# Two transformer blocks on one core: the adaLN weight tiles join the weight stream, the attention pipeline gets one unit deeper, and transposed probabilities alternate between two PSUM banks

## The reference, cut to what matters

```
for i in range(DEPTH):                                   # 2 layers
    m_lat = (jax.nn.silu(c) @ ada_w[i] + ada_b[i])[:, None, :]
    m_ctx = jax.nn.silu(c_ctx) @ ada_w[i] + ada_b[i]
    sh1, sc1, g1, sh2, sc2, g2 = jnp.split(m_lat, 6, axis=-1)
    h = _rms(x, norm1_g[i]) * (1.0 + sc1) + sh1          # the same for ctx
    # layer 0: Fourier mix and window attention (8 heads); layer 1: neighbourhood attention (16 heads)
    x = x + g1 * o
    h = _rms(x, norm2_g[i]) * (1.0 + sc2) + sh2
    x = x + g2 * _swiglu(h, ffn_w_gate[i], ffn_w_up[i], ffn_w_down[i])
```

## Time and profile before

| | us |
|---|---|
| three runs | 3373.81, 3312.71, 3373.85 (median 3373.81) |
| the profiled execution | 3314.83 |
| its span, first to last instruction | 3312.9 |
| PE busy | 3073.7 (93%) |
| DVE, ACT busy | 1651.8 (50%), 1531.3 (46%) |
| mean granted clock | 0.911 |

### The profile page before, as it was taken

One profiled execution on the slowest core, in us unless ns is written; L12 is line 12 of the kernel. 1 busy time (PEld: TensorE's weight loads), 2 busy tenths in 40 slices (PEclk: granted clock), 3 DMA queues, 4 the chain that ended last, 5 costly groups with the idle time before them and its releaser, 6 DMA issues.

```text
span 3312.9 us, 56503 instructions
## 1 busy us (share of the span) xinstructions
PE 3073.7 (93%) x22864; PEld 2946.2 (89%) x22864; DVE 1651.8 (50%) x2222; ACT 1531.3 (46%) x1890; POOL 332.9 (10%) x416
## 2 busy tenths in 40 slices
PE   6889998999999999999899978999999899999998
PEld 5777997799998789998899967999999899998998
DVE  5754445354454344474444685445444444644543
ACT  5754544355454245344354455534444454343552
POOL 0000210011002101021211000100000011204020
PEclk9986998599997579999999898998999899899899
DMA  8941543035446225543445312553323155334352
GB/s 313 334 155 52 177 178 127 1 139 180 157 147 126 15 82 185 181 163 114 153 152 178 139 53 89 181 184 131 115 99 131 52 175 180 140 128 143 137 188 104
DMA packets 65327, 470.07 MB, mean 142 GB/s; under 512 B 7584, under 2 KB 7584, under 8 KB 8736
## 3 DMA queue, kind: packets, MB, share of 16 engines
q1 hardware_dynamic: 63648, 464.85, 39.0%
q0 software_dynamic: 1536, 3.15, 1.6%
HBM read 466.92 MB, written 1.05 MB: 141 GB/s over the span
## 4 chain that ended last, share of the span: by engine, by line
PE 89%; DVE 6%; ACT 2%; DMA 1%; issue 1%; POOL 0%; SPq 0%; POOLq 0%; DVEq 0%; ACTq 0%
PE ps L487 18%; PE ps L488 18%; PE ps L489 18%; PE ps L667 5%; PE ps L515 5%; PE ps L517 4%; PE ps L516 4%; PE ps L696 4%; PE ps L553 3%; PE ps L678 3%; PE ps L530 2%; DVE cv L1468 2%; PE ps L557 1%; PE ps L807 1%; PE ps L536 1%
## 5 line engine op out<-in xcount | busy, mean ns | idle before, releaser
L1146 DVE TENSOR_TENSOR w_lo<-w_raw,w_hi 128x2048 fp32r<-128x2048 f32 x435 | 1001.7, 2303 | 879.4 <-ACT w_hi L871 878.6
L871 ACT ACTIVATE w_hi<-w_raw 128x2048 fp32r<-128x2048 f32 x437 | 835.6, 1913 | 490.7 <-PE ps L489 454.9
L487 PE MATMUL ps<-H_hi,w_hi 128*128 128x256 f32 x3424 | 985.7, 288 | 44.1 <-DVE H_lo L1220 13.5
L488 PE MATMUL ps<-H_lo,w_hi 128*128 128x256 f32 x3424 | 982.4, 287 | 0.0
L489 PE MATMUL ps<-H_hi,w_lo 128*128 128x256 f32 x3424 | 981.7, 287 | 0.0
L487 PEld LDWEIGHTS ps<-H_hi,w_hi 128*128 128x128 f32 x3424 | 671.6, 196 | 54.8 <-issue 34.2
L488 PEld LDWEIGHTS ps<-H_lo,w_hi 128*128 128x128 f32 x3424 | 671.5, 196 | 0.0
L489 PEld LDWEIGHTS ps<-H_hi,w_lo 128*128 128x128 f32 x3424 | 670.7, 196 | 0.0
L487 PE MATMUL ps<-A_hi,w_hi 128*128 (+1 forms) x1488 | 416.4, 280 | 27.2 <-POOL A_lo L1533 15.4
L488 PE MATMUL ps<-A_lo,w_hi 128*128 (+1 forms) x1488 | 415.0, 279 | 0.0
L489 PE MATMUL ps<-A_hi,w_lo 128*128 (+1 forms) x1488 | 414.7, 279 | 0.0
(11 more groups left out here) (196 smaller groups left out, 3437.5 us busy)
## 6 DMA issues: line engine op xcount, KB each, us to landing
w_raw<-weights_dram SPq DMA_DIRECT2D x437, 1024.0 KB, 4.8
bias_raw<-rel_bias_dram POOLq DMA_DIRECT2D x32, 96.0 KB, 5.9
consts<-consts_in_dram SPq DMA_DIRECT2D x1, 3010.0 KB, 10.0
Y<-ctx_in_dram SPq DMA_DIRECT2D x1, 1024.0 KB, 12.0
X<-x_in_dram SPq DMA_DIRECT2D x1, 1024.0 KB, 14.1
out_dram<-X SPq DMA_DIRECT2D x1, 1024.0 KB, 3.8
params<-params_in_dram SPq DMA_DIRECT2D x1, 361.0 KB, 3.2
```

The source lines that it names most:

```text
L487: mm(out, whi[:, cols], hi, start=first, stop=False, skip_group_check=True)
L488: mm(out, whi[:, cols], lo, start=False, stop=False, skip_group_check=True)
L871: return nc.scalar.activation(*a, **k)
L1146: V.tensor_tensor(w_lo[:, slot, :], w_raw[:, slot, :], whole(w_hi)[:, slot, :], ALU.subtract).then_inc(lo_done, 1)
```

## The change

Three edits, and one that goes with them.

1. The 48 ada tiles are no longer a phase of their own. Eight stand at the start (`ada`, `count=8`), enough for the first two sections of layer 0. The other 40 are put between other tiles of the stream: 8 in the context `qkv`, 8 in the context `attend`, 11 in the context `ffn_a`, 5 in the latent `qkv`, 8 in the latent `attend`. `ada_end` adds the bias for the sections that are complete, in three places.
2. An ada tile is no longer split. PE multiplies `w_raw` itself in float32, 8 products of 256 columns with 32 stationary columns, four of them into four separate groups of 32 PSUM partitions (`ada_rows_of`), and the two products that turn the rows now have 128 rows (`ada_cols_of`). The slot of `w_raw` is free when these products end. ACT's copy (`ada_row_of`) has 128 partitions instead of 4.
3. `attend` gets one unit deeper: scores(i), turn_p(i-2), weigh(i-3), with three buffers of `prob`, eight of `small`, ACT's copy ahead of its exponential, and `probT` of the dilated attention in `Y`. In the context, window and neighbourhood attention `turn_p(u)` writes bank 4 + u % 2 and waits for the copy of unit u-2 instead of u-1.
4. The loops of `in_loop` and `gemm_b` and `ffn_a` on PE are written out.

The core of the diff:

```diff
-        add("ada", l=l)
-        at["t"] += 24
-        at["ada"] += 1
+    add("ada", count=8)
+    stream(*[("ada", 0)] * 8)
+    add("ada_end", l=0, sections=(0, 1), which=0)
     for who in ("ctx", "lat"):
+        ctx = who == "ctx"
         norm(who, "ada", l=0, which=0)
-        qkv([("f", 0), ("f", 1), ("q", 0), ("q", 1), ("k", 0)], which="ev", who=who)
+        qkv([("f", 0), ("f", 1), ("q", 0), ("q", 1), ("k", 0)], lambda o: ("ev_in", o),
+            (1, 2, 1, 2, 2) if ctx else (1, 1, 1, 1, 1), which="ev", who=who)
         add("fourier")
         at["fo"] += 4
-        attend("ev", 16, who=who, banks=2)
-        gemm_b("H", 8, "gate", who=who, l=0, g=2)
+        attend("ev", 16, with_ada=8, who=who, banks=2)
+        if ctx:
+            add("ada_end", l=0, sections=(2, 3, 4, 5), which=1)
+        gemm_b("H", 8, "gate", ("ev_out", 0), who=who, l=0, g=2)
         norm(who, "ada", l=0, which=1)
-        ffn()
-        gemm_b("A", FC, "gate", who=who, l=0, g=5)
+        ffn("ffn0", 11 if ctx else 0)
+        gemm_b("A", FC, "gate", ("ffn0", FC), who=who, l=0, g=5)
+    add("ada_end", l=1, sections=range(6), which=None)
     norm("ctx", "ada", l=1, which=0)
...
-        c_wide = over("c_wide", 0, [P, C, P], F32R)
-        ada_rows = over("ada_rows", 8, [4, RING, 256])
+        c_wide = over("c_wide", 58, [P, C, 32])
+        ada_rows = over("ada_rows", 56, [P, 2, 256])
...
-        prob_a = over("prob", 48, [P, 2, 3 * T])
+        prob_a = over("prob", 48, [P, 3, 2 * T])
...
+        prob_d = over("prob_d", 56, [P, 3, 3 * T])
+        probT_d = Y[:, 0:6, :].rearrange("p (u c) t -> p u (c t)", u=2)
...
         def in_loop(eng, n, step):
 
-            full = n // RING if n >= 2 * RING else 0
-            if full:
-                with eng.Fori(0, full) as i:
-                    for j in range(RING):
-                        step(i, j)
-            for o in range(full * RING, n):
+            for o in range(n):
...
+            for t, (_, place, _) in enumerate(tiles):
+                if t >= RING:
+                    kind, _, o = tiles[t - RING]
+                    if kind == "ada":
+                        sp.wait_ge(tile_done, t - RING + 2)
+                    else:
+                        sp.wait_ge(lo_done, o + 1)
+                sp.dma_start(w_raw[:, t % RING, :], weights[place]).then_inc(loaded[t % RING], 16)
...
+            def ada_rows_of(t, bank):
+                m = tiles[t][2]
+                pe.wait_ge(loaded[t % RING], (t // RING + 1) * 16)
+                for k in range(C):
+                    j = k % 4
+                    last = mm(ps[32 * j:32 * j + 32, bank, 0:256], c_wide[:, k, :],
+                              w_raw[:, t % RING, k * 256:k * 256 + 256], start=k < 4, stop=k >= 4)
+                last.then_inc(tile_done, 1)
+                return m
+
+            def ada_cols_of(m, bank):
+                pe.wait_ge(ada_row, m + 1)
+                for c in range(2):
+                    last = mm(ps[:, bank, 2 * c:2 * c + 2], ada_rows[:, m % 2, c * P:c * P + P],
+                              con("add_parts"), start=True, stop=True)
+                last.then_inc(ada_col, 1)
...
-                    pe.wait_ge(ada_row, at + 1)
-                    for c in range(2):
-
-                        last = mm(ps[:, 3 + slot, 2 * c:2 * c + 2], ada_rows[:, slot, c * P:c * P + P],
-                                  con("add_parts")[0:4, :], start=True, stop=True)
-                    last.then_inc(tile_done, 1)
-                in_loop(pe, 24, step)
+                for j in range(ph["count"] + 1):
+                    if j < ph["count"]:
+                        if j >= 2:
+                            pe.wait_ge(ada_row, j - 1)
+                        ada_rows_of(ph["at"]["t"] + j, j % 2)
+                    if j >= 1:
+                        if j >= 3:
+                            pe.wait_ge(ada_evac, j - 2)
+                        ada_cols_of(j - 1, 2 + (j - 1) % 2)
 
             def norm(ph):
                 n = ph["at"]["n"]
...
                 def turn_p(u):
                     pe.wait_ge(p_exp, u0 + u + 1)
-                    if u >= 1:
-                        pe.wait_ge(pt_copy, u0 + u)
+                    apart = which != "dil"
+                    if u >= 1 + apart:
+                        pe.wait_ge(pt_copy, u0 + u - apart)
                     for k in range(blocks):
-                        last = nc.tensor.transpose(ps[:, 4 + k // 4, (k % 4) * P:(k % 4) * P + P],
-                                                   prob[:, u % 2, k * P:k * P + P], ident)
+                        bank = 4 + u % 2 if apart else 4 + k // 4
+                        last = nc.tensor.transpose(ps[:, bank, (k % 4) * P:(k % 4) * P + P],
+                                                   prob[:, u % 3, k * P:k * P + P], ident)
                     last.then_inc(pt_done, 1)
 
...
+                columns = None
+                for i in range(n + 3):
                     if i < n:
                         scores(i)
-                    if 1 <= i <= n:
-                        turn_p(i - 1)
-                    if i >= 2:
-                        weigh(i - 2)
+                    if columns is not None:
+                        ada_cols_of(columns, 3)
+                        columns = None
+                    if 2 <= i <= n + 1:
+                        turn_p(i - 2)
+                    if i >= 3:
+                        weigh(i - 3)
+                    if i % 2 == 1 and i // 2 < ph["with_ada"]:
+                        t = ph["at"]["t"] + i // 2
+                        if i >= 3:
+                            pe.wait_ge(ada_evac, tiles[t][2])
+                        columns = ada_rows_of(t, 1)
...
             def split(ph, i, j):
 
-                t0 = ph["at"]["t"] + AHEAD
-                tile = t0 + RING * i + j
-                if isinstance(tile, int) and tile >= NT:
+                tile = ph["at"]["t"] + AHEAD + RING * i + j
+                if tile >= NT or tiles[tile][0] == "ada":
                     return
-                slot = (t0 + j) % RING
-                act.wait_ge(loaded[slot], ((t0 + j) // RING + i + 1) * 16)
+                slot = tile % RING
+                act.wait_ge(loaded[slot], (tile // RING + 1) * 16)
                 act.wait_ge(tile_done, tile - 1)
                 A(w_hi[:, slot, :], w_raw[:, slot, :], ACT.Copy).then_inc(hi_done, 1)
+
+            def ada_row_of(t, bank):
+                m = tiles[t][2]
+                act.wait_ge(tile_done, t + 2)
+                if m >= 2:
+                    act.wait_ge(ada_col, m - 1)
+                A(ada_rows[:, m % 2, :], ps[:, bank, 0:256], ACT.Copy).then_inc(ada_row, 1)
 
...
-                prob = prob_d if which == "dil" else prob_a
+                prob, turned = (prob_d, probT_d) if which == "dil" else (prob_a, probT)
                 width = {"ev": 4 if ph["who"] == "lat" else 2, "od": 4, "dil": 6}[which] * P
-                for u in range(n + 1):
+                for u in range(n + 2):
+                    if u >= 2:
+                        w = u - 2
+                        act.wait_ge(pt_done, u0 + w + 1)
+                        if w >= 2:
+                            act.wait_ge(o_done, u0 + w - 1)
+                        src = ps[:, 4:6, :].rearrange("p b f -> p (b f)") if which == "dil" else ps[:, 4 + w % 2, :]
+                        A(turned[:, w % 2, 0:width], src[:, 0:width], ACT.Copy).then_inc(pt_copy, 1)
                     if u < n:
-                        s = small[:, (u0 + u) % 4]
+                        s = small[:, (u0 + u) % 8]
                         act.wait_ge(s_max, u0 + u + 1)
                         if which == "ev":
-                            A(prob[:, u % 2, 0:width], prob[:, u % 2, 0:width], ACT.Exp, bias=s[:, 2:3],
+                            A(prob[:, u % 3, 0:width], prob[:, u % 3, 0:width], ACT.Exp, bias=s[:, 2:3],
                               accum_out=s[:, 3:4])
                             A(s[:, 4:5], par("sink", u // 2), ACT.Exp, bias=s[:, 2:3]).then_inc(p_exp, 1)
                         else:
-                            A(prob[:, u % 2, 0:width], prob[:, u % 2, 0:width], ACT.Exp, bias=s[:, 2:3],
+                            A(prob[:, u % 3, 0:width], prob[:, u % 3, 0:width], ACT.Exp, bias=s[:, 2:3],
                               accum_out=s[:, 3:4]).then_inc(p_exp, 1)
-                    if u >= 1:
-                        w = u - 1
-                        act.wait_ge(pt_done, u0 + w + 1)
-                        if w >= 2:
-                            act.wait_ge(o_done, u0 + w - 1)
-                        A(probT[:, w % 2, 0:width], ps[:, 4:6, :].rearrange("p b f -> p (b f)")[:, 0:width],
-                          ACT.Copy).then_inc(pt_copy, 1)
+                    if u % 2 == 1 and u // 2 < ph["with_ada"]:
+                        split(ph, 0, u // 2)
```

352 lines of the change are left out of this document (192 added, 160 removed).

## The result

The changed kernel takes 3219.38 us (median of four runs, 3216.06 to 3221.11), the kernel before beside it 3309.03 to 3373.85. The ratio of the two is 0.9714, with a 95% interval from 0.9692 to 0.9736, and leaves out the two longer runs of the kernel before (3373.81 and 3373.85): faster, but by little more than half of what I forecast. The profiled execution took 3218.66 us with a span of 3216.9, against 3314.83 and 3312.9: -96.

A forecast was written before the change was run, and what follows sets the result against it. PE, busy 93% of the span, was taken as the bound, with weak clock in three attention stages. Terms -135 + 16 + 6 + 26 - 69 - 14 + 3 - 2 = -169 us from 3314.8 gave 3146 us; eight in ten 3085 to 3300.

The forecast's parts named there:

- The start: Start up to the first norm: with eight unsplit ada tiles there, the norm starts at about 50 us instead of 185.0, -135 us.
- The neighbourhood attention: Neighbourhood attention: the deeper order keeps PE at the high clock, 81 us against 150, -69 us.
- neighbourhood slow: Rival: the neighbourhood attention stays at 1.2 GHz, +69 us, total 3215; chance 0.13.
- both together: Rival: context, window and neighbourhood attention all at the low clock, total 3311, no change; chance 0.12.
- The context and window attention: Context and window attention with ada tiles, at the high clock by the deeper order: +3 and -14 us.
- context and window slow: Rival: both attentions fall to 1.2 GHz as ada products and load waits break the rhythm, +39 and +57, total 3242; chance 0.14.
- The dilated term: Dilated attention: same banks and 3.58 us a unit, the 1 us stall gone in each half, -2 us.
- The latent q/k/v term: Latent q/k/v with five ada tiles: 12 us of PE against 12 us idle, other tiles' splits delayed, +6 us.
- The price of an ada tile: Ada tile moved into other stages: 1.9 us of products plus 0.5 of columns, 2.4 us of PE (1.4 to 4.5).
- no overlap: Rival: the ada products' column groups do not overlap, 2.1 us more a tile, +85 us, total 3231; chance 0.10.
- Full overlap: Ada products: all four column groups overlap, 1 us less a tile, total 3111; counted within the forecast's chance of 0.44.
- Loops at nothing: PE's loops written out: 0 us, bounds -3 to +5.

The follow-up runs named there:

- x4: Changed kernel with the old attention order and one pair of banks in all attentions, ada tiles left in place: 3268.94, 3269.53, 3317.54 and 3321.20 us.
- x5: Changed kernel with the deeper order kept but the alternation of banks for transposed probabilities undone: 3226.62 and 3228.87 us.
- x6: Changed kernel with all 48 ada tiles back at the start, still with the new unsplit products: 3249.47 and 3252.67 us.
- x16: Changed kernel plus products meant for the ffn ahead of the dilated norms, which never ran: 3176.53, 3179.18, 3194.97, and 3220.64 to 3236.17 us three times.
- x1: Changed kernel with the old order in the dilated attention alone: 3238.15, 3230.69, 3228.32 and 3178.84 us.
- x9: Changed kernel with the five ada tiles of the latent q/k/v moved to the latent ffn: 3164.78, 3167.49, 3169.38, 3211.10 and 3213.22 us.
- x7: Changed kernel with all eight products of an ada tile in one group of 32 partitions instead of four groups: 3298.96 and 3302.99 us.
- x8: Changed kernel with PE's loops of three tiles put back in gemm_b: 3219.90 and 3223.68 us.
- x13: Changed kernel plus eight unused float32 products of one column at the first tile of the first dilated q/k/v: 3172.82 to 3179.67 us.
- x3: Changed kernel plus eight unused float32 products of 128 columns behind the first tile of the first dilated q/k/v: 3174.50 us, ratio to before 0.9531.

## Why the prediction was wrong

**The sum was right in its two large gains.** The start, -138 against -135, by the steps named. The neighbourhood attention, -69.5 against -69: the chain of mask, maximum and exponential no longer stops PE at the entry (a gap of 0.7 us and one of 0.3 are left, as forecast), and the clock stays at 1.00. x4 shows that it is the order that does this. That also settles the rival "neighbourhood slow" and with it "both together". The part of the argument that gave the second bank a share is wrong: x5 has the same 193 us without it.

The context and window attention came out at +3 and -19 against +3 and -14, but the step behind them is only half right. The deeper order was to keep the clock in both. In the context attention it doesn't by itself (0.56 in x6), and with the tiles the clock is at 0.86; in the window attention it isn't needed (0.94 in x4). The rival "context and window slow" had the ada tiles break the rhythm, and where they stand the clock is higher. The +3 looks partly like luck: a tile costs less than I had put, and the low stretch takes time back.

**The dilated term failed: "same banks, same 3.58 us, its one 1 us stall gone in each half: -2".** It was +46, 48 of the 73 us between forecast and measurement. The term holds for a high run (387.1 against 389.6 us in the profile of x16), but nine of the changed kernel's first ten runs were low. I had the price in hand (57 us for a half at 1.2 GHz, 49 between the two profiles) and had guessed that the longer runs of before are such a half; I then wrote that "the deeper start makes that rarer". That step is what failed. No run shows the order to have a part in it: with the old one, x1 was low in three of four runs and x4 in two. The gap of 0.73 us stood at the entry before the change as well, and removing the stall of 1.0 us behind it did not keep the clock. What made the low half commoner than the 18 longer runs in 48 of before, if that is what they are, stays open. The spread of before's runs should have given this case a chance of its own: the same state at 57 us would have put 3203 next to 3146.

**The latent q/k/v term failed: +6 against +21.8.** I let one tile fill the 9.2 us wait of the earlier trace rows and took the ring for deep enough. In the chain an ada tile's products, then 4.85 + 1.92 + 2.29 us of load and splits, come ahead of the tile three places later, while the stage has only one gemm tile of PE between two ada tiles; the waits for staged tiles grew from 12 to 21 us. x9 took the tiles out and got 24.4 us back. The context q/k/v has the same (a load of 6.82 us and its two splits, 1.92 and 2.30, in the chain from 68.75 on); I had put 2 us on it there, and +16 became +25.4: PE is idle 12 of 62 us, against 5 of 37, and the clock is at 0.86.

**The price of an ada tile was mis-sized.** I took 1.9 + 0.5 us from the rule that only the second record of a product overlaps. All four groups overlap: 1.00 + 0.34 us at the high clock, 1.87 + 0.94 at the low one. The rival "no overlap" (3231) has a total near the measured one and is nevertheless wrong; x7 is that case, and it is 82 us slower still. "Full overlap" had the groups right, and its sum is 3106, not 3111 (1 us less on 40 tiles). The context ffn came out at +22.4 against +26 partly by two errors: eleven tiles cost 14.7 us in products, 1.5 in a wait for ACT's copy of the last, and the remaining 6 are spread over the stage and the second product (64.9 us against 61.7), without a wait that the profile names.

**Loops at nothing** was right for `gemm_b` (x8); for `ffn_a` no run tells. The latent ffn of layer 0 and all other stages taken together grew by 12 us, at a pace of 87 products in 10 us instead of 91 in the one that I looked into (x8); what sets that pace stays open.

## What to carry to other kernels

When the fastest and the slowest run of a kernel differ by about the price of one stage at the other clock, take that stage as a term of the sum with two values until a profile of a long run says otherwise. An edit ahead of it may change how often each comes, and a handful of runs of one kind doesn't settle it: four of four low here became twelve of 16. Filling the entry's gap with unused products gave ten of ten high. And see that an added instruction is in the trace before its run is read: the products of x16 were not. A tile that is used unsplit frees its slot only when its products end: put such tiles where PE has long work between two of them (an ffn), not where the next load's splits decide. Ask of each part of a combined change what it does alone: here the order gave 71 us in one stage and 90 in all, the spreading 32, the four groups instead of one 82, and the second bank nothing.

## What the runs showed of the hardware

Sixteen float32 records of 256 columns with 32 stationary columns take 3.57 us in one column group (x7) and 1.00 us over four, both with records of 379 ns.

A float32 product with one moving column takes as long as one with 128: 0.11 us for each of its two records (x13 and x3).

PE at 1.2 GHz with no idle time stayed there for the whole first dilated half (1.00 busy, 0.50, 174 records in 50 us), while the same instructions at 2.4 GHz stayed there too (347 records in 50 us in the second).

One and the same kernel had the first half at either clock in different executions, with the same gap of 0.73 us at the same place: changed kernel and x16, 435.9 and 387.1 us for the dilated part.

In the start of x6 the granted clock is recorded as 1.00, and yet each record lasts 631 ns, which is the low level's duration (379 at the high one), with PE busy 97.89 of 100 us. Ahead of the first record of the clock (at 181.8 us in that trace) durations tell the level, and not that column:

```profile
60.00:160.00 100.00, 97.89 (x700) 52.86 (x692) 7.33 (x35) 15.22 (x36) 0.00 (x0) 1.00 0.97 373
```
